# Head norms of the first block with tokens on partitions, half of one modulation sum on TensorE, the recurrent convolution accumulated in PSUM

## The chip, the cores and the metric

The kernel runs on one core of a Trainium2 chip. The metric is the device time of one execution in microseconds (us), taken as the median of several. TensorE is called PE in the profile, its weight load PEld, VectorE DVE, ScalarE ACT, GpSimd POOL and SyncE SP.

## The reference

Two transformer-like blocks run on 512 tokens of width 1024. The change lies wholly in the first part of the first block, ahead of its output projection:

```python
c_act = jax.nn.silu(c)
ada = c_act @ w_ada[l] + b_ada[l]
sh1, sc1, g1, sh2, sc2, g2 = jnp.split(ada, 6, axis=-1)
h = modulate(rmsnorm(x, norm1_g[l]), sh1, sc1)
z = h @ w_in[l]
gate_b, gate_c, xa, xr, gr = jnp.split(z, [CONV_W, 2 * CONV_W, 3 * CONV_W, 3 * CONV_W + LRU_W], axis=-1)
y_a = gate_b * causal_dwconv(gate_c * xa, conv_a_w[l])
xr = causal_dwconv(xr, conv_b_w[l]) + conv_b_b[l]
y_b = rg_lru(xr, w_r[l], b_r[l], w_i[l], b_i[l], lru_lambda[l]) * jax.nn.gelu(gr)
y = jnp.concatenate([head_rmsnorm(y_a, gn_a[l], N_CONV_HEADS),
                     head_rmsnorm(y_b, gn_b[l], N_LRU_HEADS)], axis=-1) @ w_out[l]
x = x + g1[:, None, :] * y
...
def head_rmsnorm(y, g, n_heads):
    yh = y.reshape(b, s, n_heads, w // n_heads).astype(jnp.float32)
    yh = yh * lax.rsqrt(jnp.mean(yh * yh, axis=-1, keepdims=True) + EPS)
    return yh.reshape(b, s, w).astype(y.dtype) * g
```

There are 16 heads of 64 channels, eight from each half. An expert layer with 16384 experts and a second block follow; nothing in them changes.

## The kernel before

**Layout and precision.** Activations lie with channels on the 128 partitions and the 512 tokens along the row. Width 1024 makes eight chunks of 128 channels, so a chunk of `y` holds two heads. Every large product is done in three passes: operand and weight are each split into a rounded upper part (`act_hi`, `w_hi`) and the rest (`act_lo`, `w_lo`).

**Units.** A unit is one block of 128 output channels: 24 matmuls of 512 columns (`linear`, L876; eight chunks by three passes). Its weights come by DMA into `raw`, ACT makes `w_hi` (`upper_part`, L1228, up to two units ahead), POOL makes `w_lo` (`lower`, L782). Units 0 to 19 are the projection `w_in`: 0 to 3 give `xr`, 4 to 7 `gr`, and 8 to 19 go round in threes (`z_of`, L643): `xa`, `gc` (gate_c), `gb` (gate_b). Units 20 to 27 are `w_out`.

**Order.** Each engine runs its own program strictly in the order written, and waits on semaphores. No scheduler reorders anything. PE, ACT and DVE each have a loop over the unit number u; numbers in tuples (`Y_SQUARE`, `Y_SUM`, `Y_SCALE`) say at which u a step of head chunk i is placed. These positions differ in time from engine to engine, since an engine can lag behind another by some units.

**Modulation sums.** The six vectors of `ada` are made in twelve halves. `weighted(h)` (L1623) on DVE sums eight products of a 128x512 piece of `w_ada` by a scalar into `acc`; `ada_half(h)` (L909) on PE turns `acc` into four columns with four matmuls against a column of ones. Halves 0 to 3 come before unit 0, half 4 after unit 3, half 5 after unit 5 (`ADA_AFTER`), 6 to 9 in the output projection. `ada_done` counts the finished halves.

**Recurrent half.** DVE convolves `xr` with four taps into `xc` (L1681, L1683), PE makes the two gates of chunk g after unit 5+g (L943, L944), ACT takes tanh, DVE does `recur_1(g)` (L1690, with one full reciprocal) at u=8 to 11, ACT takes four square roots, and DVE does `recur_2(g)` (L1704, with the scan, L1708) at u=13 to 16, which gives `y[4+g]`.

**Convolution half.** For each m, DVE multiplies `gc` by `xa` (L1727), convolves with three taps (L1731, L1733) and multiplies by `gb` (L1737), at u = 9, 12, 15, 18 and u = 10, 13, 16, 19.

**Head norm of chunk i** (order `Y_ORDER`): ACT squares `y` (L1242); PE multiplies the squares by the matrix `halves`, which sums each head over its 64 partitions and leaves the sum on every partition of the head, 128x512 (`squares`, L893, L902); ACT takes the root (L1248); DVE takes the reciprocal of all 128x512 elements (`invert`, L1589, L1594) and scales `y` (`scale_y`, L1711, L1718); ACT makes `act_hi` (`y_upper`, L1312, L1314) and DVE `act_lo` (L1755). On PE, the only step of this chain is the sum; what DVE does with it is awaited by PE only in that the next sum needs the root before (`rms_ready`) and in unit 20, chunk by chunk (`split=8`). After the eighth chunk DVE goes on to `weighted(6)`.

## Time and profile before

| | us |
|---|---|
| median of 3 runs | 2073.28 |
| the three runs | 2069.87, 2073.28, 2074.01 |
| the profiled execution | 2072.42 |
| its span, first to last instruction | 2070.7 |
| mean granted PE clock | 0.958 |
| PE busy / DVE busy | 1885.8 / 1673.6 |

The profiled execution took 0.86 us less than the median, and 1.7 us of it lie outside the span. All instants below are counted from the start of the span. The part that the change touches ends at about 217 us, a tenth of the span. The rest runs after it without a change: its first work needs what this part makes.

### The profile page before, as it was taken

What the parts mean: (1) busy time and instruction counts of PE and PEld (TensorE: products, weight loads), DVE (VectorE), ACT (ScalarE), POOL (GpSimd) and SP (SyncE); (2) the same over time, 40 slices, a digit from 0 to 9 for tenths busy, and PEclk for the clock granted to TensorE, in tenths of its full rate; (3) what the DMA queues carried; (4) which work ended last, traced back from release to release, by engine and by line L of the source; (5) the groups of instructions that cost most, each with busy time, mean ns of one, the idle gap of its engine ahead of it and who ended that gap; (6) DMA issues with size and microseconds to landing.
All of it is one profiled execution on the core that took longest, in us unless ns stands there. A gap on an engine that the chain in (4) does not pass through costs nothing. (4 is left out here: it accounts for less than half of the span.)

```text
span 2070.7 us, 27489 instructions
## 1 busy us (share of the span) xinstructions
PE 1885.8 (91%) x9551; PEld 1612.7 (78%) x9551; DVE 1673.6 (81%) x2614; ACT 712.8 (34%) x1101; POOL 1057.4 (51%) x654
## 2 busy tenths in 40 slices
PE   3997779999999999996699999999999888899996
PEld 2774558999998999996678787878787666788774
DVE  6889874999968888865789999999997977646646
ACT  2343134333334444432233333333334233233441
POOL 1332234555556556567777777777754622432102
PEclk7998789999999999998899999999999999999988
DMA  8241342555458889989999999999982221100011
GB/s 331 86 170 41 132 153 64 177 174 177 167 173 309 310 304 319 314 317 414 376 352 369 354 363 359 368 356 358 370 299 79 72 71 62 61 1 1 1 51 51
DMA packets 160807, 440.37 MB, mean 213 GB/s; under 512 B 13648, under 2 KB 63952, under 8 KB 157648
## 3 DMA queue, kind: packets, MB, share of 16 engines
q1 hardware_dynamic: 65296, 254.71, 34.6%
q0 software_dynamic: 36864, 134.23, 16.7%
q10 hardware_dynamic: 58560, 50.34, 7.4%
q8 instruction: 46, 0.75, 0.1%
q14 instruction: 41, 0.34, 0.0%
HBM read 386.80 MB, written 52.43 MB: 212 GB/s over the span
## 5 line engine op out<-in xcount | busy, mean ns | idle before, releaser
L786 POOL TENSOR_TENSOR w_lo<-raw,w_hi 128x1024 fp32r<-128x1024 f32 x300 | 724.8, 2416 | 835.7 <-ACT w_hi L1237 834.9
L1237 ACT ACTIVATE w_hi<-raw 128x1024 fp32r<-128x1024 f32 x332 | 351.7, 1059 | 973.6 <-PE PS L887 594.6
L887 PE MATMUL PS<-act_hi,w_hi 128*128 128x384 f32 (+1 forms) x1632 | 608.5, 373 | 72.5 <-POOL w_lo L786 38.9
L887 PE MATMUL PS<-act_hi,w_lo 128*128 128x384 f32 (+1 forms) x1632 | 592.0, 363 | 0.0
L887 PE MATMUL PS<-act_lo,w_hi 128*128 128x384 f32 (+1 forms) x1632 | 591.9, 363 | 0.0
L887 PEld LDWEIGHTS PS<-act_hi,w_hi 128*128 128x128 f32 x1632 | 315.5, 193 | 129.2 <-issue 38.5
L887 PEld LDWEIGHTS PS<-act_lo,w_hi 128*128 128x128 f32 x1632 | 314.7, 193 | 26.6
L887 PEld LDWEIGHTS PS<-act_hi,w_lo 128*128 128x128 f32 x1632 | 316.1, 194 | 24.5 <-issue 1.4
L1043 PE MATMUL PS<-w_hi,act_hi 128*128 128x512 f32 x768 | 302.6, 394 | 15.8 <-ACT arena L1353 6.7
L1043 PE MATMUL PS<-w_hi,act_lo 128*128 128x512 f32 x768 | 300.2, 391 | 0.0
L1043 PE MATMUL PS<-w_lo,act_hi 128*128 128x512 f32 x768 | 300.1, 391 | 0.0
L1925 DVE TENSOR_TENSOR act_lo<-arena,act_hi 128x384 fp32r<-128x384 f32 x128 | 236.9, 1851 | 32.7 <-ACT act_hi L1405 32.4
L1887 DVE CUSTOM_DVE_ANT_0 arena<-arena,PS 128x1024 f32<-128x1024 f32 x128 | 154.6, 1217 | 46.6 <-DMA arena<-in_expert_u_rows,arena 45.6
L1043 PEld LDWEIGHTS PS<-w_hi,act_hi 128*128 128x128 f32 x768 | 144.8, 189 | 56.2 <-issue 19.0
L1043 PEld LDWEIGHTS PS<-w_hi,act_lo 128*128 128x128 f32 x768 | 144.7, 188 | 30.7
L1043 PEld LDWEIGHTS PS<-w_lo,act_hi 128*128 128x128 f32 x768 | 145.0, 189 | 28.9
L1896 DVE SCALAR_TENSOR_TENSOR PS<-arena,PS 128x1024 f32<-128x1024 f32 x127 | 162.4, 1279 | 1.7
L832 POOL DMA_INDIRECT arena<-in_expert_v,arena x128 | 135.0, 1054 | 26.1 <-issue 20.7
L1877 DVE TENSOR_TENSOR arena<-PS,arena 128x1024 f32<-128x1024 f32 x96 | 117.2, 1221 | 35.6 <-PE PS L1006 29.9
L832 POOL DMA_INDIRECT arena<-in_expert_u_rows,arena x128 | 123.0, 961 | 29.9 <-issue 22.7
L1069 PEld LDWEIGHTS PS<-arena 128*128 128x128 f32 x752 | 89.1, 194 | 19.6 <-issue 10.1
L1069 PE MATMUL PS<-arena 128*128 128x128 f32 x752 | 94.9, 281 | 6.1 <-POOL arena L870 4.9
(309 smaller groups left out, 2074.4 us busy)
## 6 DMA issues: line engine op xcount, KB each, us to landing
raw<-in_expert_u SPq DMA_DIRECT2D x128, 512.0 KB
raw<-in_expert_v SPq DMA_DIRECT2D x128, 512.0 KB
raw<-in_w_in SPq DMA_DIRECT2D x52, 512.0 KB
arena<-in_w_ada SPq DMA_DIRECT2D x24, 1024.0 KB, 6.8
gel_d<-arena ACTq DMA_DIRECT2D x64, 384.0 KB
gates_d<-arena ACTq DMA_DIRECT2D x12, 2048.0 KB
arena<-gates_d SPq DMA_DIRECT2D x32, 768.0 KB
arena<-gel_d SPq DMA_DIRECT2D x32, 768.0 KB
```

The source lines that it names most:

```text
L786: pool.tensor_tensor(w_lo[:, k % SPLIT, :], raw[:, k % RAW, :], w_hi[:, k % SPLIT, :].bitcast(F32), ALU.subtract).then_inc(lo_split, 1)
L832: pool.indirect_dma_start(out=rows[buffer(s)], out_offset=None, in_=table, in_offset=bass.IndirectOffsetOnAxis(ap=row_i[:, s % SLOTS:s % S ...
L887: mm = pe.matmul(PS[:, bank, 0:n_tok], w[:, k % SPLIT, c * P:(c + 1) * P], x[:, c, 0:n_tok], start=(i == 0 and n == 0), stop=(i == KC - 1 ...
L1043: mm = pe.matmul(PS[:, 2 * q + half, :], coef(x, k)[:, q, :], w[:, k % SPLIT, own], start=(start and n == 0), stop=(stop and n == 2), skip ...
L1069: mm = pe.matmul(PS[:, b, h * P:(h + 1) * P], lhs(h), rhs(h), start=True, stop=True)
L1237: act.activation(w_hi[:, k % SPLIT, :], raw[:, k % RAW, :], ACT.Copy).then_inc(hi_split, 1)
L1877: chain.link(v.tensor_tensor(hot[:, n, :, :], numbers.unsqueeze(1).unsqueeze(1).to_broadcast([P, GROUP, 2, P]), routeT[:, 0:2, at].rearran ...
L1887: v.tensor_tensor_reduce(out=rows[buffer(s)], in0=rows[buffer(s)], in1=own_ps, scale=1.0, scalar=0.0, op0=ALU.mult, op1=ALU.add, accum_out ...
L1896: v.scalar_tensor_tensor(out=own_ps, in0=rows[buffer(s)], scalar=dots[:, k:k + 1], in1=own_ps, op0=ALU.mult, op1=ALU.add).then_inc(rows_us ...
L1925: v.tensor_tensor(coef(act_lo, b % 4), craw[:, b % 2, :].rearrange("p (q t) -> p q t", q=GT), coef(act_hi, b % 4).bitcast(F32), ALU.subtra ...
```

## The change

Four things change.

1. **Head norms.** PE now multiplies with the squares as the stationary operand and two columns of `halves` as the moving one: four matmuls of 2 columns for each chunk (`head_sum`), so the sums have tokens on the partitions and are 128x8. ACT's root and DVE's reciprocal become 128x8 (`head_root`, `head_invert`). Then ACT copies the 8 values out to 128x512 (`spread`), PE turns that back to channels on partitions with four matmuls of 128 columns against the identity (`head_spread`), and DVE scales `y` with that straight from PSUM. `head_spread(i)` stands in PE's program at `Y_INV[i]`, the u at which DVE had its reciprocal, and waits for ACT's `spread(i)`, which waits for DVE's `head_invert(i)`. DVE scales one step later.
2. **Half 2 of the modulation.** DVE sums four of its eight products; PE does the other four straight from the weights with 16 matmuls of one column, and DVE adds the two with one small instruction.
3. **Recurrent convolution.** The sum of the four taps lies in PSUM (banks 3, 4, 7, 7) until the last one writes `xc`.
4. **Order.** Convolutions 0 and 1 come ahead of `weighted(4)`, 2 and 3 ahead of `weighted(5)`. PE takes half 4 after unit 5 and half 5 after unit 7. The gates wait for two and four convolutions in place of one and two. The last lower parts of `y` are interleaved with the last scalings.

The core of the diff (semaphores, two small regions and SP's count of freed pieces are left out):

```diff
-        ADA_AFTER = {3: 4, 5: 5, U_OUT + 1: 6, U_OUT + 2: 7, U_OUT + 3: 8, U_OUT + 4: 9, U_Q + 2: 10, U_Q + 4: 11}
+        PE_SHARE = (2,)
+        ADA_AFTER = {5: 4, 7: 5, U_OUT + 1: 6, U_OUT + 2: 7, U_OUT + 3: 8, U_OUT + 4: 9, U_Q + 2: 10, U_Q + 4: 11}
...
-        Y_SCALE = (13, 16, 17, 18, 19, 20, 20, 20)
+        Y_INV = (13, 16, 17, 18, 19, 20, 20, 20)
...
+            def head_sum(i):
+
+                index, n = 1 + i, 8 + i
+                if index >= 2:
+                    pe.wait_ge(rms_ready, index - 1)
+                pe.wait_ge(sq_ready, n + 1)
+                pair = halves[:, :].rearrange("p (a b) -> p a b", a=2)[:, :, 0]
+                for q in range(TB):
+                    mm = pe.matmul(PS[:, 6 + index % 2, 2 * q:2 * q + 2], sq[:, n % 2, q * P:(q + 1) * P], pair,
+                                   start=True, stop=True)
+                mm.then_inc(sq_used, 1)
+                pe.wait_ge(sq_used, n + 1)
+                pe.nop().then_inc(sum_ready, 1)
+
+            def head_spread(i):
+
+                pe.wait_ge(spread_ready, i + 1)
+                if i >= 2:
+                    pe.wait_ge(y_scaled, i - 1)
+                for q in range(TB):
+                    mm = pe.matmul(PS[:, 3 + i % 2, q * P:(q + 1) * P], tmp[:, i % 2, q * P:(q + 1) * P], ident[:, :],
+                                   start=True, stop=True)
+                mm.then_inc(spread_ps, 1)
+
             def ada_half(h):
+                if h in PE_SHARE:
+                    pe.wait_ge(ada_in[(2 * h + 1) % 4], 16 * ((2 * h + 1) // 4 + 1))
+                    pe.wait_ge(c_ready, 1)
+                    for n in range(4):
+                        for c in range(4, KC):
+                            at = 512 * (c % 4) + n * P
+                            own = 40 + 4 * h + n
+                            mm = pe.matmul(PS[:, 5, own:own + 1], ada_w[:, (2 * h + 1) % 4, at:at + P], cs[:, c:c + 1],
+                                           start=(c == 4), stop=(c == KC - 1))
+                    mm.then_inc(ada_used_pe, 1)
...
@@ -932,7 +979,7 @@
...
-                    pe.wait_ge(xc_ready, g + 1)
+                    pe.wait_ge(xc_ready, (2, 4, 4, 4)[g])
...
                 for i in range(8):
                     if Y_SUM[i] == u:
-                        squares(8 + i, 1, 1 + i, halves)
-            for i in range(8):
-                if Y_SUM[i] == 20:
-                    squares(8 + i, 1, 1 + i, halves)
+                        head_sum(i)
+                    if Y_INV[i] == u:
+                        head_spread(i)
+            head_sum(6)
+            head_spread(5)
+            head_sum(7)
+            head_spread(6)
+            head_spread(7)
...
+            def head_root(i):
+                act.wait_ge(sum_ready, 2 + i)
+                if i >= 1:
+                    act.wait_ge(rinv_ready, i)
+                act.activation(hrms[:, i % 2, :], PS[:, 6 + (1 + i) % 2, 0:8], ACT.Sqrt, bias=eps,
+                               scale=1.0 / 64).then_inc(rms_ready, 1)
+
+            def spread(i):
+
+                act.wait_ge(rinv_ready, 2 + i)
+                if i >= 2:
+                    act.wait_ge(spread_ps, i - 1)
+                act.activation(tmp[:, i % 2, :].rearrange("p (a b) -> p a b", b=64),
+                               hinv[:, i % 2, :].unsqueeze(2).to_broadcast([P, 8, 64]), ACT.Copy).then_inc(spread_ready, 1)
...
                 for i in range(8):
                     if Y_SUM[i] == u:
-                        root(1 + i, 64)
+                        head_root(i)
+                    if Y_INV[i] == u:
+                        spread(i)
...
-            for i in range(5):
+            y_upper(0)
+            spread(5)
+            for i in range(1, 4):
                 y_upper(i)
-            root(7, 64)
-            y_upper(5)
-            root(8, 64)
-            y_upper(6)
-            y_upper(7)
+            head_root(6)
+            spread(6)
+            y_upper(4)
+            head_root(7)
+            spread(7)
+            for i in range(5, 8):
+                y_upper(i)
...
-                for c in range(KC):
+                for c in range(4 if h in PE_SHARE else KC):
...
             chain.link(v.tensor_tensor(ada[:, 0:16], PS[:, 5, 0:16], col("bada", 0, 16), ALU.add))
+            chain.link(v.tensor_tensor(ada[:, 8:12], PS[:, 5, 48:52], ada[:, 8:12], ALU.add))
             chain.link(v.scalar_tensor_tensor(out=gain1, in0=ada[:, 8:16], scalar=1.0, in1=col("n1", 0, 8),
                                               op0=ALU.add, op1=ALU.mult))
...
             for m in range(4):
-                if m < 2:
-                    weighted(4 + m)
                 dve.wait_ge(z_act, m + 1)
                 if m == 0:
                     dve.wait_ge(pool_made, 2)
                 w = [col("cbw", 4 * k + m) for k in range(4)]
-                chain.link(v.tensor_scalar(xc[:, m, :], xrp[:, m, 0:512], w[0], col("cbb", m), ALU.mult, ALU.add))
+                part = PS[:, (3, 4, 7, 7)[m], :]
+                if m == 3:
+                    dve.wait_ge(xc_ready, 3)
+                chain.link(v.tensor_scalar(part, xrp[:, m, 0:512], w[0], col("cbb", m), ALU.mult, ALU.add))
                 for k in range(1, 4):
-                    ins = v.scalar_tensor_tensor(out=xc[:, m, :], in0=xrp[:, m, k:k + 512], scalar=w[k],
-                                                 in1=xc[:, m, :], op0=ALU.mult, op1=ALU.add)
+                    ins = v.scalar_tensor_tensor(out=xc[:, m, :] if k == 3 else part, in0=xrp[:, m, k:k + 512], scalar=w[k],
+                                                 in1=part, op0=ALU.mult, op1=ALU.add)
                     if k < 3:
                         chain.link(ins)
                     else:
                         ins.then_inc(xc_ready, 1)
+                if m % 2:
+                    weighted(4 + m // 2)
...
+            def head_invert(i):
+
+                dve.wait_ge(rms_ready, 2 + i)
+                if i >= 2:
+                    dve.wait_ge(spread_ready, i - 1)
+                v.reciprocal(hinv[:, i % 2, :], hrms[:, i % 2, :]).then_inc(rinv_ready, 1)
+
             def scale_y(i):
 
                 c = Y_ORDER[i]
-                if i:
-                    invert(1 + i, i, y_scaled)
-                else:
-                    invert(1, 8)
-                v.scalar_tensor_tensor(out=y[:, c, :], in0=y[:, c, :], scalar=col("gn", c), in1=rinv, op0=ALU.mult,
-                                       op1=ALU.mult).then_inc(y_scaled, 1)
+                dve.wait_ge(spread_ps, i + 1)
+                v.scalar_tensor_tensor(out=y[:, c, :], in0=y[:, c, :], scalar=col("gn", c), in1=PS[:, 3 + i % 2, :],
+                                       op0=ALU.mult, op1=ALU.mult).then_inc(y_scaled, 1)
+
+            def lower_y(i):
+
+                dve.wait_ge(ahi_ready, 8 + i + 1)
+                v.tensor_tensor(act_lo[:, Y_ORDER[i], :], y[:, Y_ORDER[i], :], act_hi[:, Y_ORDER[i], :].bitcast(F32),
+                                ALU.subtract).then_inc(alo_ready, 1)
...
                 for i in range(8):
-                    if Y_SCALE[i] == u:
-                        scale_y(i)
+                    if Y_INV[i] == u:
+                        head_invert(i)
+                        if i:
+                            scale_y(i - 1)
...
-            for i in range(8):
-                if Y_SCALE[i] == 20:
-                    scale_y(i)
-
-                dve.wait_ge(ahi_ready, 8 + i + 1)
-                v.tensor_tensor(act_lo[:, Y_ORDER[i], :], y[:, Y_ORDER[i], :], act_hi[:, Y_ORDER[i], :].bitcast(F32),
-                                ALU.subtract).then_inc(alo_ready, 1)
+            head_invert(5)
+            scale_y(4)
+            for i in range(0, 3):
+                lower_y(i)
+            head_invert(6)
+            scale_y(5)
+            lower_y(3)
+            head_invert(7)
+            scale_y(6)
+            lower_y(4)
+            scale_y(7)
+            for i in range(5, 8):
+                lower_y(i)
```

On PE, from the head sum behind unit 12 to the one behind unit 15. L887 and L900 are the matmuls of a unit, of which only the first is shown, since it carries the unit's waits; `sq_ready` comes from ACT's square, `z_act` and `z_dve` free the unit's PSUM bank. Before:

```order
L902 MATMUL PS<-arena 128x512 [waits sq_ready,gates_th]
L887 MATMUL PS<-act_hi,w_hi 128x512 [waits sq_used,lo_split,z_dve]
...
L887 MATMUL PS<-act_hi,w_hi 128x512 [waits lo_split,z_act]
...
L887 MATMUL PS<-act_hi,w_hi 128x512 [waits lo_split,z_dve]
...
L902 MATMUL PS<-arena 128x512 [waits sq_ready,rms_ready]
L887 MATMUL PS<-act_hi,w_hi 128x512 [waits sq_used,lo_split,z_dve]
```

After (L930 is `head_sum`, L942 `head_spread`):

```order
L930 MATMUL PS<-arena 128x2 [waits sq_ready,gates_th]
L930 MATMUL PS<-arena 128x2 x3
L900 MATMUL PS<-act_hi,w_hi 128x512 [waits sq_used,lo_split,z_dve]
...
L942 MATMUL PS<-ident,arena 128x128 [waits spread_ready]
L942 MATMUL PS<-ident,arena 128x128 x3
L900 MATMUL PS<-act_hi,w_hi 128x512 [waits lo_split,z_act]
...
L900 MATMUL PS<-act_hi,w_hi 128x512 [waits lo_split,z_dve]
...
L930 MATMUL PS<-arena 128x2 [waits sq_ready,rms_ready]
L930 MATMUL PS<-arena 128x2 x3
L900 MATMUL PS<-act_hi,w_hi 128x512 [waits sq_used,lo_split,z_dve]
```

Behind unit 13 PE now has four matmuls that wait for `spread_ready`, and units 14 and 15 stand behind them.

On DVE, from the last product of `gb` 1 (L1737 before, L1823 after) to the next `gc`, where the first head norm is; L1707 to L1709 and L1783 to L1785 are `recur_2`. Before:

```order
L1737 TENSOR_TENSOR arena<-PS,arena 128x512 [waits unit_done,dve_chain]
L1707 TENSOR_TENSOR arena<-arena 128x512 [waits z_dve,root_ready]
L1708 SCALAR_TENSOR_TENSOR arena<-arena 128x512 [waits dve_chain]
L1709 TENSOR_TENSOR arena<-arena 128x512 [waits dve_chain]
L1594 RECIPROCAL arena<-arena 128x512 [waits tmp_ready,rms_ready]
L1718 SCALAR_TENSOR_TENSOR arena<-arena,cols 128x512 [waits rinv_ready]
L1707 TENSOR_TENSOR arena<-arena 128x512 [waits root_ready]
L1708 SCALAR_TENSOR_TENSOR arena<-arena 128x512 [waits dve_chain]
L1709 TENSOR_TENSOR arena<-arena 128x512 [waits dve_chain]
L1727 TENSOR_TENSOR arena<-PS,arena 128x512 [waits dve_chain,z_act,unit_done]
```

After:

```order
L1823 TENSOR_TENSOR arena<-PS,arena 128x512 [waits unit_done,dve_chain]
L1783 TENSOR_TENSOR arena<-arena 128x512 [waits z_dve,root_ready]
L1784 SCALAR_TENSOR_TENSOR arena<-arena 128x512 [waits dve_chain]
L1785 TENSOR_TENSOR arena<-arena 128x512 [waits dve_chain]
L1792 RECIPROCAL arena<-arena 128x8 [waits rms_ready]
L1783 TENSOR_TENSOR arena<-arena 128x512 [waits root_ready]
L1784 SCALAR_TENSOR_TENSOR arena<-arena 128x512 [waits dve_chain]
L1785 TENSOR_TENSOR arena<-arena 128x512 [waits dve_chain]
L1813 TENSOR_TENSOR arena<-PS,arena 128x512 [waits dve_chain,z_act,unit_done]
```

The large reciprocal and its scaling are gone from this place; a small reciprocal stands in it, still behind `recur_2(0)`, and the scaling of this chunk comes behind `recur_2(3)`.

## Rows read from the trace of the kernel before

**Rows 1.** stretches: us, PE, PEld, DVE, ACT, POOL busy (count), PE clock, DMA, GB/s

```profile
75.00:82.00 7.00, 6.02 (x23) 4.96 (x24) 6.50 (x7) 1.18 (x2) 2.38 (x1) 0.76 0.34 112
...
108.00:148.00 40.00, 39.70 (x169) 31.21 (x167) 35.56 (x29) 16.83 (x23) 14.07 (x7) 1.00 0.43 149
148.00:176.00 28.00, 25.37 (x103) 18.85 (x102) 26.86 (x22) 8.04 (x11) 12.21 (x5) 1.00 0.28 95
176.00:184.00 8.00, 4.19 (x9) 2.34 (x10) 7.79 (x6) 3.36 (x5) 2.36 (x1) 0.79 0.04 4
...
198.00:217.00 19.00, 9.19 (x22) 6.30 (x23) 16.81 (x14) 2.86 (x5) 0.00 (x0) 0.59 0.00 1
```

**Rows 2.** DVE, 119 to 217 us, by line: count | busy us, mean ns | idle

```profile
L1594 DVE RECIPROCAL arena<-arena 128x512 f32<-128x512 f32 x8 | 26.8, 3348 | 0.4 <-DVE arena L1737 0.2
```

**Rows 3.** DVE in order: start us, us, line, what, count [idle before <-releaser]

```profile
119.43 0.69 DVE L1727 TENSOR_TENSOR arena<-PS,arena 128x512 f32<-128x512 f32 x1 [2.81 <-PE PS L887]
...
146.26 3.53 DVE L1733 SCALAR_TENSOR_TENSOR arena<-arena,cols 128x512 f32<-128x512 f32 x2
...
154.50 3.35 DVE L1594 RECIPROCAL arena<-arena 128x512 f32<-128x512 f32 x1
...
215.98 0.69 DVE L1755 TENSOR_TENSOR act_lo<-arena,act_hi 128x512 fp32r<-128x512 f32 x1 [0.69 <-ACT act_hi L1314]
```

**Rows 4.** PE in order, same columns

```profile
75.98 1.05 PE L912 MATMUL PS<-ones,arena 128*128 128x1 f32 x8 [1.46 <-DVEq L1640]
...
142.18 0.39 PE L887 MATMUL PS<-act_lo,w_hi 128*128 128x512 f32 x1
...
147.62 0.39 PE L887 MATMUL PS<-act_lo,w_hi 128*128 128x512 f32 x1
...
179.51 1.75 PE L902 MATMUL PS<-arena 128*128 128x512 f32 x2 [3.85 <-ACT arena L1242]
```

**Rows 5.** DVE in the start

```profile
26.44 5.59 DVE L1635 SCALAR_TENSOR_TENSOR arena<-arena,small 128x512 f32<-128x512 f32 x7
32.27 3.35 DVE L1594 RECIPROCAL arena<-arena 128x512 f32<-128x512 f32 x1 [0.24 <-DVE arena L1635]
35.66 1.34 DVE L1633 TENSOR_SCALAR arena<-arena,small 128x512 f32<-128x512 f32 x1
```

**Rows 6.** POOL in order, the splits into w_lo

```profile
32.06 4.66 POOL L786 TENSOR_TENSOR w_lo<-raw,w_hi 128x1024 fp32r<-128x1024 f32 x2 [27.93 <-ACT w_hi L1237]
...
146.79 5.26 POOL L786 TENSOR_TENSOR w_lo<-raw,w_hi 128x1024 fp32r<-128x1024 f32 x2 [7.42 <-ACT w_hi L1237]
```

**Rows 7.** DVE, convolutions 0, 1 and 2, and a small reciprocal

```profile
58.29 0.18 DVE L1579 RECIPROCAL small<-small 128x4 f32<-128x4 f32 x1
...
76.09 2.34 DVE L1681 TENSOR_SCALAR arena<-arena,cols 128x512 f32<-128x512 f32 x1 [0.32 <-DVE arena L1635]
...
89.66 4.33 DVE L1683 SCALAR_TENSOR_TENSOR arena<-arena,cols 128x512 f32<-128x512 f32 x3
...
94.48 2.33 DVE L1683 SCALAR_TENSOR_TENSOR arena<-arena,cols 128x512 f32<-128x512 f32 x3
```

**Rows 8.** DVE, expert stage, 1060 to 1500 us, by line: operations with PSUM and without

```profile
L1925 DVE TENSOR_TENSOR act_lo<-arena,act_hi 128x384 fp32r<-128x384 f32 x106 | 197.7, 1865 | 23.1 <-ACT act_hi L1405 22.9
L1896 DVE SCALAR_TENSOR_TENSOR PS<-arena,PS 128x1024 f32<-128x1024 f32 x114 | 145.8, 1279 | 1.6
...
L1900 DVE TENSOR_SCALAR PS<-arena 128x1024 f32<-128x1024 f32 x1 | 1.3, 1289 | 0.1
```

**Rows 9.** PE, second block: 16 passes of 128 columns, at either clock

```profile
1766.43 1.95 PE L1069 MATMUL PS<-arena 128*128 128x128 f32 x16
...
1808.33 3.50 PE L1069 MATMUL PS<-arena 128*128 128x128 f32 x16 [4.87 <-POOL arena L870]
```

**Rows 10.** ACT, 0 to 230 us, by line

```profile
L1237 ACT ACTIVATE w_hi<-raw 128x1024 fp32r<-128x1024 f32 x24 | 25.4, 1057 | 77.0 <-PE PS L887 72.8 <-DMA raw<-in_w_in 4.3
...
L1242 ACT ACTIVATE arena<-arena 128x512 f32<-128x512 f32 x8 | 5.0, 625 | 3.1 <-DVEq L1739 3.1
```

More of the change, by code:

```diff
@@ L291, in build @@
         rinv = region("rinv", 27672, 1, 512)[:, 0, :]
+        hrms = region("hrms", 30040, 2, 8)
+        hinv = region("hinv", 30056, 2, 8)
         lru_q = region("lru_q", 28184, 1, 512)[:, 0, :]
@@ L401, in build @@
         ada_used = sem("ada_used")
+        ada_used_pe = sem("ada_used_pe")
         ada_acc = sem("ada_acc")
@@ L436, in build @@
         y_scaled = sem("y_scaled")
+        spread_ready = sem("spread_ready")
+        spread_ps = sem("spread_ps")
         x_ready = sem("x_ready")
@@ L628, in lowered, with piece_used @@
             return lo_split, u + 1 - N_KEYS // 4
+        def piece_used(i):
+            if i % 2 and i // 2 in PE_SHARE:
+                return ada_used_pe, PE_SHARE.index(i // 2) + 1
+            return ada_used, sum(1 for n in range(i + 1) if not (n % 2 and n // 2 in PE_SHARE))
         def coef(x, k):
@@ L660, in ada_half @@
                     if i >= 4:
-                        sp_.wait_ge(ada_used, i - 3)
+                        sp_.wait_ge(*piece_used(i - 4))
                     sp_.dma_start(ada_w[:, i % 4, :], A["w_ada"][h][:, 2048 * (i % 2):2048 * (i % 2) + 2048]
```

## The prediction

> **What bounds the kernel now.** The stage table [rows 1] comes first. From 108 to 176 us PE and DVE both look full: PE is busy 39.70 of 40 us and DVE 35.56, then 25.37 and 26.86 of 28. Behind 176 us PE has holes and DVE none: 4.19 us of PE against 7.79 of DVE in 8 us, and from 198 to 217 us 9.19 against 16.81, with PE's granted clock down to 0.59. So DVE sets the end of this part. The list of DVE's groups says with what: eight reciprocals of 128x512 at 3348 ns, 26.8 us in all [rows 2]. DVE in order of time gives the instants: it last waits for PE at 119.43 us, comes to the first head reciprocal at 154.50 and ends its last lower part at 215.98 + 0.69 = 216.67 us [rows 3]. That end is my yardstick. Four sums `weighted(6)` to `weighted(9)` follow on DVE at once and pace the output projection, so a shift of this instant passes to the end of the program; nothing behind it is changed.
>
> PE in order of time gives the other half. A unit takes 147.62 - 142.18 = 5.44 us, and unit 13 ends at 142.4 us [rows 4]. DVE comes to the head reciprocal that belongs to unit 13's place only at 154.50 [rows 3]. **PE runs 12 us ahead of DVE there.** Today this lead costs nothing: PE goes on with units 14 and 15, and DVE finds them done.
>
> **The start (half 2).** DVE drops four of eight products; seven take 5.59 us [rows 5], so 4 x 0.80 = 3.2 us. But POOL makes its first two splits at 32.06 us, 4.66 us for both [rows 6], and before they ran beside the reciprocal at 32.27 us, which they don't slow; only the next instruction lost time, 1.34 us against about 0.5 [rows 5]. Moved 3.2 us forward, `weighted(3)` starts under these splits. One split costs a product with two SBUF operands about 2 us: three convolution steps took 4.33 us with a split beside them and 2.33 without [rows 7]. Two splits cost about 4 us in place of 0.85, which eats the 3.2. The added small instruction costs 0.2. PE's 16 products are 32 passes, at 1.05 / 8 us each [rows 4] 4.2 us, twice that at half clock, and PE has from 27 to 43 us for them. I take 0 for the start, with -3.2 (no collision) and +0.4 as its ends.
>
> The Trainium skill (SBUF — State Buffer, SBUF: two separate sides) says that GpSimd and a VectorE operation with two SBUF inputs, or in a two-port mode, lock each other out for the whole instruction. By that rule the start gains 0, without it 3.2 us; the convolution rows just named agree with the rule.
>
> **Convolutions in PSUM and the new order.** A step with one operand in PSUM isn't held up by POOL: 114 of 1024 columns average 1279 ns in a stage where the product without PSUM takes 1865 ns for 384 columns [rows 8]. Half of 1279 is 0.64 us, near the 0.78 of an undisturbed step now [rows 7]. The first step rises from about 0.55 to 1289 / 2 = 0.64 us [rows 8], and two stalls of 2 us on DVE go [rows 7]. None of it is on the path by itself, because DVE waits for PE behind the convolutions.
>
> The Trainium skill (VectorE: DVE Perf Modes, Why PSUM operands drop a tier) speaks against the first step: a PSUM operand excludes the mode with two reads. By the page it doubles from about 0.5 us; by the rows it costs 0.1 us more, 0.4 us for four.
>
> What counts is the order. PE waits 1.46 us for half 4 behind unit 3 [rows 4], and its clock then falls: 0.76 over the next 7 us [rows 1] is 1.7 us lost. With the half behind unit 5 DVE has it ready (about 82 us, PE asks at 85.5), and the gates find their convolutions (DVE at 73.5 and 88, PE at 86 and 93.5). **Gain 3.2 us**: unit 9 ends at 116.2 us in place of 119.4, unit 13 at 139.2. Ends: 1.5 to 3.5.
>
> **The head norms.** DVE loses 8 x (3.35 - 0.2) = 25.2 us; 0.2 is a small reciprocal [rows 7]. Prices of the new chain, all hot: small reciprocal 0.25 with its wait, ACT's copy 0.63 [rows 10], 0.7 with its wait; `head_spread` is 8 passes of 128 columns, 16 took 1.95 us [rows 9], so 1.1 with its wait; `head_sum` is 8 passes of 2 columns, like the 1.05 of [rows 4], with its own wait 1.3 (today also about 1.3); ACT's small root 0.3.
>
> `head_spread(0)` stands behind unit 13 on PE and waits for DVE's `head_invert(0)`, still behind `recur_2(0)`. Queued behind it are units 14 and 15, which DVE needs for `gc` 2. ACT waits too, in `spread`, with its split for unit 16 behind. In turn:
>
> 1. DVE starts `gc` 0 at 116.2. Up to the reciprocal it needed 154.50 - 119.43 = 35.1 us [rows 3], with two POOL splits in it [rows 6]; one of them now can't come, since ACT is stuck: 33. `head_invert(0)` at 149.3, `head_spread(0)` at 150.2. **PE idle 11 us** (9 to 13).
> 2. Spread 1.1, units 14 and 15 10.9: 162.2. DVE did `recur_2(1)` in 2.6 us and idled 10.
> 3. `gc` 2: 2.8 and 2.0 for a split (two steps took 3.53 beside one, 1.5 without [rows 3, 6]): 167.0. `recur_2(2)` 169.6. PE: sum 1.3, unit 16: 169.0. `gb` 2 and `recur_2(3)` with a partial stall 5.1: 174.7. Invert and copy: 175.7. PE idle 6.7.
> 4. Spread, sum, unit 17: 1.1 + 1.3 + 5.5: 183.6. ACT first splits weights (1.06 [rows 10]) and copies `xa`, then spreads: 185.8. PE idle 2.2.
> 5. Spread, sum, unit 18: 193.7. DVE idled about 14 us. `gc` 3 with a split 4.8, invert and copy 0.9: 199.4. PE idle 5.7.
> 6. Spread, sum, unit 19: 207.3; `gb` 3 and invert: 208.4.
> 7. Tail: three rounds of invert, copy, spread, sum, root, 3.65 each, and 3.3 for the last scaling and lower parts: **222.7 us**.
>
> Against 216.67 this is +6.0 us with PE always at full clock. DVE gave up 25.2 us of work and got more than 34 us of waiting.
>
> **The clock.** 3.85 us of idleness ahead of 179.51 [rows 4] went with a clock of 0.79 over 8 us [rows 1]: 1.7 us lost, as above. Four stalls: 4 x 1.7 = 6.8. In the tail two PE steps a round take 3.50 / 1.95 of their time at the lower of the two levels (1.2 of 2.4 GHz) [rows 9], about 0.8 more each, six steps: 4.7; I take half, 2.3. **Sum: +6.0 + 6.8 + 2.3 = +15 us** on the profiled 2072.4, so 2087.5; the median lay 0.9 above the profiled execution, and the cold share of the second and third stall may overlap, so I say 2087 for the median.
>
> **Rivals.** *The reciprocals' time comes through* (faster). If DVE reached `head_invert(0)` before 139.2 us, PE would never wait. PE's own floor is 139.2 + 6 x 5.5 + 8 x (1.3 + 1.1) = 191.4 us, 196 with the last lower parts: -21 us, 2052. For it: 26.8 us of reciprocals are truly on DVE's path [rows 2]. Against it: DVE would have to be 10 us earlier at `recur_2(0)`, and nothing ahead of that place gets shorter but the 3.2 us that PE gains as well. 5%. Part of it (short stalls, -4 to -15 us) 4%.
>
> *The waits replace the gain, nothing more* (no change). With sum and spread at half their prices (0.5 each less, eight times each, some 6 of them on the path: -6), a start that gains its 3.2 and a PE that keeps its clock, the sum is between -3 and +3: 2070 to 2077. 11%.
>
> *Coupled more tightly* (slower still). Every spread and sum at half clock (+0.8 each on about 12) and a POOL split in each `recur_2`: +22 to +28, 2095 to 2101. 13%.
>
> My forecast (+4 to +22, 2077 to 2095) has 67%. The change not doing what it says isn't a case: each of the moved instructions stands in the new order.
>
> **Numbers.** About 0.2% (4 us) is what a measurement of this kernel can tell from no change. Faster 0.09; within 0.2% 0.11; slower 0.80. The range leaves out the faster case and the far end of the tight one: 2074 to 2097.
>
> **What would show it.** In the profile after: PE idle ahead of `head_spread` 0, 1 and 3, released by ACT's copy, 11, 7 and 6 us; DVE idle ahead of `gc` 2, `gc` 3 and `gb` 3 that wasn't there; small reciprocals of 0.2 us; unit 9 about 3 us earlier than now; `weighted(2)` half as long and `weighted(3)` slowed by POOL; PE's clock under 0.85 in the slices from 150 to 215 us; last lower part at about 231 us. It is wrong if `head_spread(0)` finds its data, if DVE is busy between 150 and 195 us, or if unit 13 ends later than `recur_2(0)`.

## The result and the profile after

| | before | after |
|---|---|---|
| median, us | 2072.47 (4 runs, 2069.87 to 2074.01) | 2093.6 (4 runs, 2092.01 to 2096.89) |
| profiled execution, us; its span | 2072.42; 2070.7 | 2096.89; 2095.2 |
| ratio | | 1.0105, 95% interval 1.0088 to 1.0123 |
| last lower part of the head norms ends (DVE) | 216.67 | 234.85 + 1.89 = 236.74 (DVE's next instruction, at 236.65, overlaps it a little) |

The change makes the kernel 21 us slower. The profiled execution is the slowest of the four; of the 24.5 us between it and the one of before, 20.1 stand at the yardstick instant of the prediction (the end of DVE's last lower part). The unchanged part behind that instant took 1854.0 us before and 1858.5 after, and between 1851.0 and 1856.9 in the profiled executions below; so a median can lie some us off what its yardstick says. The stage table of the kernel after, columns as in [rows 1]:

```profile
75.00:82.00 7.00, 7.00 (x32) 5.80 (x31) 6.71 (x6) 3.08 (x4) 3.40 (x2) 1.00 0.34 111
108.00:148.00 40.00, 30.61 (x135) 24.40 (x133) 32.84 (x30) 15.90 (x22) 14.40 (x6) 0.94 0.37 126
148.00:176.00 28.00, 19.94 (x88) 16.56 (x88) 15.87 (x16) 5.49 (x8) 7.15 (x3) 0.87 0.17 47
176.00:192.00 16.00, 12.10 (x40) 9.97 (x40) 2.39 (x6) 3.18 (x6) 0.64 (x1) 0.64 0.08 31
192.00:208.00 16.00, 9.48 (x41) 7.72 (x42) 5.60 (x6) 2.76 (x5) 4.05 (x2) 0.79 0.19 60
208.00:222.00 14.00, 11.84 (x51) 10.06 (x50) 1.58 (x4) 2.47 (x4) 1.93 (x1) 0.74 0.02 7
222.00:237.00 15.00, 13.34 (x58) 12.60 (x58) 8.63 (x16) 7.88 (x16) 0.42 (x1) 0.55 0.01 1
```

Where [rows 1] had a full DVE, DVE now works 15.87 of 28 us, then 2.39 of 16, 5.60 of 16 and 1.58 of 14. PE isn't full either, and its granted clock lies between 0.55 and 0.87. Neither engine bounds this stretch; they wait for each other in turn. In the first row, which had 0.76 before, the granted clock is 1.00: PE's wait for half 4 behind unit 3 is gone. PE's side, its five waits ahead of the spreading passes (in brackets the idle time ahead of a row, and who ended it):

```profile
150.51 2.08 PE L942 MATMUL PS<-ident,arena 128*128 128x128 f32 x8 [11.60 <-ACT arena L1314]
...
177.71 2.08 PE L942 MATMUL PS<-ident,arena 128*128 128x128 f32 x8 [6.95 <-ACT arena L1314]
...
192.34 1.16 PE L942 MATMUL PS<-ident,arena 128*128 128x128 f32 x8 [2.23 <-ACT arena L1314]
...
207.67 2.07 PE L942 MATMUL PS<-ident,arena 128*128 128x128 f32 x8 [5.88 <-ACT arena L1314]
...
220.68 1.16 PE L942 MATMUL PS<-ident,arena 128*128 128x128 f32 x8 [1.86 <-ACT arena L1314]
```

DVE's side, in order of time: the product sums at the start, a convolution in PSUM, `gc` 0 (it answers to 119.43 in [rows 3]), the first head inverse, `gc` 2, `gc` 3, `gb` 3, the last three lower parts:

```profile
34.65 7.54 DVE L1707 SCALAR_TENSOR_TENSOR arena<-arena,small 128x512 f32<-128x512 f32 x7
...
84.17 0.81 DVE L1755 TENSOR_SCALAR PS<-arena,cols 128x512 f32<-128x512 f32 x1 [0.25 <-DVE arena L1707]
85.02 1.55 DVE L1757 SCALAR_TENSOR_TENSOR PS<-arena,cols,PS 128x512 f32<-128x512 f32 x2
...
115.82 0.69 DVE L1813 TENSOR_TENSOR arena<-PS,arena 128x512 f32<-128x512 f32 x1 [5.92 <-PE PS L900]
...
149.61 0.19 DVE L1792 RECIPROCAL arena<-arena 128x8 f32<-128x8 f32 x1
...
163.99 0.69 DVE L1813 TENSOR_TENSOR arena<-PS,arena 128x512 f32<-128x512 f32 x1 [11.64 <-PE PS L900]
...
201.83 0.69 DVE L1813 TENSOR_TENSOR arena<-PS,arena 128x512 f32<-128x512 f32 x1 [19.30 <-PE PS L900]
...
218.86 0.69 DVE L1823 TENSOR_TENSOR arena<-PS,arena 128x512 f32<-128x512 f32 x1 [11.29 <-PE PS L900]
...
234.85 1.89 DVE L1804 TENSOR_TENSOR act_lo<-arena,act_hi 128x512 fp32r<-128x512 f32 x3
```

DVE is 3.6 us early at `gc` 0, comes to the first inverse without a wait, and then idles 11.64, 19.30 and 11.29 us for units that are queued behind PE's waits.

### The profile page after: what moved, and what is told of

It reads as the page before. It is cut to its first block, busy times and chain, and to the rows that moved or that the text cites. A ratio compares the mean times of both kernels' runs of the same rounds, so it can differ in the third digit from the quotient of the medians.

```text
span 2095.2 us, 27792 instructions
## 1 busy us (share of the span) xinstructions
PE 1905.5 (91%) x9695; PEld 1641.3 (78%) x9695; DVE 1643.9 (78%) x2611; ACT 714.2 (34%) x1109; POOL 1054.5 (50%) x654
## 4 chain that ended last, share of the span: by engine, by line
PE 70%; DVE 14%; POOL 5%; issue 5%; DMA 4%; ACT 2%; ACTq 0%; SPq 0%; DVEq 0%; PEldq 0%; POOLq 0%
PE PS L900 35%; PE PS L1094 18%; PE PS L1120 4%; PE PS L1057 4%; POOL w_lo L799 3%; DVE arena L1707 2%; POOL arena L845 2%; DVE arena L2122 2%; DMA gates_d<-arena 1%; DVE arena L1666 1%; PE PS L1266 1%; PE PS L1248 1%; DVE PS L1990 1%; DMA raw<-in_expert_u 1%; PE PS L915 1%
## 5 line engine op out<-in xcount | busy, mean ns | idle before, releaser
L900 PE MATMUL PS<-act_hi,w_hi 128*128 128x384 f32 (+1 forms) x1632 | 608.3, 373 | 59.2 <-POOL w_lo L799 37.0
L900 PE MATMUL PS<-act_hi,w_lo 128*128 128x384 f32 (+1 forms) x1632 | 593.1, 363 | 0.0
L900 PE MATMUL PS<-act_lo,w_hi 128*128 128x384 f32 (+1 forms) x1632 | 591.6, 363 | 0.0
L900 PEld LDWEIGHTS PS<-act_hi,w_hi 128*128 128x128 f32 x1632 | 316.2, 194 | 107.5 <-POOL w_lo L799 33.2
L900 PEld LDWEIGHTS PS<-act_lo,w_hi 128*128 128x128 f32 x1632 | 315.6, 193 | 26.6
L900 PEld LDWEIGHTS PS<-act_hi,w_lo 128*128 128x128 f32 x1632 | 316.1, 194 | 24.5 <-issue 1.4
L1094 PEld LDWEIGHTS PS<-w_lo,act_hi 128*128 128x128 f32 x768 | 144.7, 188 | 28.9
```

Of the source, the lines that this page charges most:

```text
L900: mm = pe.matmul(PS[:, bank, 0:n_tok], w[:, k % SPLIT, c * P:(c + 1) * P], x[:, c, 0:n_tok], start=(i == 0 and n == 0), stop=(i == KC - 1 ...
L1094: mm = pe.matmul(PS[:, 2 * q + half, :], coef(x, k)[:, q, :], w[:, k % SPLIT, own], start=(start and n == 0), stop=(stop and n == 2), skip ...
```

## The experiments

Theory: the loss is made by the place at which PE waits (its lead over DVE is given up), and is paid a second time in PE's clock. Rivals: the new small work itself is dear; the other three parts cost something; the units are late for another reason. In the table "last lower" is the end of DVE's last lower part in the profiled execution (before 216.67); ratios are to the kernel before on the same chip, with 95% intervals. The experiments ran on three chips, on which the kernel before took 2072.27, 2073.46 and 2072.30 us, so differences of about 1 us between medians of two chips mean nothing.

| kernel | median, us | ratio | last lower |
|---|---|---|---|
| changed kernel again | 2093.24 | 1.0104 (1.0087 to 1.0121) | 237.85 |
| old head norms, the other three parts | 2068.65 | 0.9985 (0.9975 to 0.9995) | 210.90 |
| new head norms alone | 2096.95 | 1.0124 (1.0107 to 1.0141) | 242.04 |
| late spreading | 2055.84 | 0.9925 (0.9903 to 0.9946) | 197.95 |
| copies of constants | 2071.12 | 0.9994 (0.9979 to 1.0009) | 218.78 |
| copies of constants, first in ACT's queue | 2054.19 | 0.9908 (0.9892 to 0.9925) | 198.72 |
| useless passes, short | 2091.94 | 1.0090 (1.0074 to 1.0105) | 233.50 |
| useless passes, full | 2081.24 | 1.0046 (1.0032 to 1.0060) | 225.23 |
| first weight split held | 2092.68 | 1.0101 (1.0086 to 1.0117) | 237.14 |
| new order alone | 2070.17 | 0.9985 (0.9976 to 0.9994) | 213.37 |
| late spreading, `weighted(6)` moved | 2056.00 | 0.9919 (0.9904 to 0.9934) | 200.47 |

**Which part costs.** The changed kernel with its norms undone, and the reverse. Of the first, the scalings on DVE (PE's and ACT's steps are put back as well):

```diff
-                    if Y_INV[i] == u:
-                        head_invert(i)
-                        if i:
-                            scale_y(i - 1)
+                    if Y_SCALE[i] == u:
+                        scale_y(i)
```

> The kernel before with half 2 shared, the convolutions in PSUM and the new order, but with the old head norms (full reciprocals, sums on all 128 partitions). My theory, that the loss is all in the head norms: gc 0 starts on DVE at about 116 us, as in the changed kernel, DVE is busy from there as before, and its last lower part ends about 3.5 us earlier than 216.67, so about 2069 us. Rival, that the lead of PE hides the earlier start or that the PSUM operands cost what they save: 2072 to 2074. Rival, that these three parts themselves carry part of the loss: above 2076.

Measured 2068.65, 3.6 us under the 2072.27 of before; `gc` 0 starts at 115.64. The three other parts gain, and gain what was forecast. The reverse, from the changed kernel:

```diff
-        PE_SHARE = (2,)
-        ADA_AFTER = {5: 4, 7: 5, ...
+        PE_SHARE = ()
+        ADA_AFTER = {3: 4, 5: 5, ...
...
-                part = PS[:, (3, 4, 7, 7)[m], :]
```

> The changed kernel with half 2, the convolutions and their order as they were before; only the head norms are new. My theory: the first stall of PE, ahead of the first spreading passes, is again 11 us, only about 3.5 us later in time, the following stalls are the same, and the whole is about 3.5 us slower than the changed kernel: 2096 to 2098 us. Rival, that the stalls come from units that arrive earlier than DVE can use them: the first stall is then about 8 us and the time stays at 2092 to 2094.

Measured 2096.95, 3.7 above the changed kernel, with PE's first wait 12.0 us and its five waits 28.9 us in all (28.5 in the changed kernel). The parts add up. The norms alone cost 24.6 us (2093.24 - 2068.65), or 24.7 against the kernel before on one chip (2096.95 - 2072.27).

**Is it the place of the wait?** Same work, spreading passes later in PE's order, copies and scalings with them, the tail interleaved to fit:

```diff
+        Y_SPREAD = (16, 17, 18, 19, 20, 20, 20, 20)
+        Y_SCALE = (17, 18, 19, 20, 20, 20, 20, 20)
...
 PE
-                    if Y_INV[i] == u:
+                    if Y_SPREAD[i] == u:
                         head_spread(i)
...
 ACT, ahead of its wait for the unit
+                for i in range(8):
+                    if Y_SPREAD[i] == u:
+                        spread(i)
```

> The changed kernel with the same work, but the spreading passes of head norm 0 stand behind unit 16 on PE in place of unit 13, those of 1 to 3 behind units 17 to 19, the others in the tail; ACT's copies and DVE's scalings move with them. My theory, that what costs is the place at which PE waits in its order and not the new work: PE has no wait above 3 us ahead of the spreading passes, its clock stays near full, unit 19 ends at about 184 us and the last lower part at 197 to 200, so 2053 to 2058 us, faster than both kernels. Rival, that the small passes and copies themselves are dear (sums and spreads at twice their price): PE is busy all through and the last lower part ends at about 215, 2070 us. Rival, that DVE again sets the end (scalings and lower parts in the tail): the last lower part at 205 to 210, 2062 to 2067.

Measured 2055.84, **16 us faster than before and 37 faster than the changed kernel**. PE in order of time in this kernel (L944 is `head_spread`):

```profile
158.21 1.06 PE L944 MATMUL PS<-ident,arena 128*128 128x128 f32 x8
...
167.45 1.16 PE L944 MATMUL PS<-ident,arena 128*128 128x128 f32 x8 [1.38 <-ACT arena L1317]
...
175.24 1.06 PE L944 MATMUL PS<-ident,arena 128*128 128x128 f32 x8
...
182.95 1.06 PE L944 MATMUL PS<-ident,arena 128*128 128x128 f32 x8
```

Of the 28.5 us of waits ahead of spreading passes 0 to 4, one of 1.38 us and a gap of 0.30 are left. The rival of dear small work falls: all of it is still there. But this kernel changes two things: PE's wait comes later, and ACT's copies stand ahead of the next weight split. Spreading passes moved on PE alone were not tried.

**Whose wait is it?** The order of the changed kernel, but ACT copies constants in place of the inverses, so the head norms are missing from the values:

```diff
-                act.wait_ge(rinv_ready, 2 + i)
...
-                               hinv[:, i % 2, :].unsqueeze(2)...
+                               col("gn", 0, 8).unsqueeze(2)...
```

> The changed kernel in its own order, but ACT's copy spreads eight columns of constants in place of the inverses that DVE makes, so it waits for nobody on DVE; the head norms are left out of the values in this way, and all instructions stay. My theory: with this one dependence gone PE's stalls ahead of the spreading passes vanish, the last lower part ends at about 198 us and the whole takes 2053 to 2060 us. Rival, that the new work itself costs the time: 2085 to 2093. Rival, that PE then stalls at the next dependence on DVE (the square of the next head tile) as long as before: 2080 or more.

Measured 2071.12, outside every expectation. PE still waits 12.2 us for the copies, though these need nothing of DVE. ACT in order of time shows why for the first of them:

```profile
134.65 1.66 ACT L1378 ACTIVATE arena<-arena 128x512 f32<-128x512 f32 x3
141.41 0.63 ACT L1378 ACTIVATE arena<-arena 128x512 f32<-128x512 f32 x1 [5.09 <-DVE arena L1776]
141.94 1.04 ACT L1288 ACTIVATE w_hi<-raw 128x1024 fp32r<-128x1024 f32 x1
142.89 0.61 ACT L1313 ACTIVATE arena<-cols 128x512 f32<-128x512 f32 x1
```

The copy (L1313) is queued behind a square root that waits for DVE's `recur_1(3)` and behind a weight split. The four later waits, 1.75 us and once 2.23, have a weight split of 1.06 us ahead of the copy, the one of 2.23 also ACT's copy of `xa`; the changed kernel has that 2.23 too, so it was none of DVE's there. So a second coupling lay under the first. Moved ahead of both (the old place is deleted):

```diff
 ACT, ahead of its wait for unit u
+                for i in range(8):
+                    if min(Y_INV[i], 20) == u + (1 if i == 0 else 0) and u < 20:
+                        spread(i)
```

> The kernel whose ACT copies spread constants (the head norms left out of the values), and in it these copies 0 to 4 moved on ACT ahead of the next weight split, copy 0 ahead of the four square roots too; PE's order is the one of the changed kernel. My theory, that what was left of PE's waits there, 12.2 us, stood behind ACT's own queue (a square root that waits for DVE, a weight split of 1.06 us): no wait above 1 us ahead of spreading passes 0 to 4, the last lower part ends at 198 to 203 in place of 218.78, 2054 to 2059 us. Rival, that PE then waits as long for another step of DVE (a bank that the product of three units earlier must free): last lower part at 212 or later, 2065 or more.

Measured 2054.19; one wait of 2.0 us is left on PE ahead of passes 0 to 4, for a bank that a scaling must free. Of the 39 us between this kernel and the changed one, the medians give 22 to the data from DVE (2093.24 - 2071.12) and 17 to ACT's queue (2071.12 - 2054.19), the last lower parts 19 and 20 (237.85, 218.78, 198.72). The kernel in the middle spreads from 2066 to 2078 us, so no finer split than about half and half is shown, and only in this order of undoing: with the real inverses in place, an earlier place in ACT's queue alone was not tried.

**What does the clock cost?** Useless passes on PE ahead of its waits:

```diff
             def head_spread(i):
+                for n in range((30, 16, 4, 14, 0, 0, 0, 0)[i]):
+                    pe.matmul(PS[:, 5, 128:256], ones[:, :], ident[:, :], start=True, stop=True)
                 pe.wait_ge(spread_ready, i + 1)
```

> The changed kernel, with 30, 16, 4 and 14 useless passes of 128 columns on PE (0.29 us each at the high clock, into a corner of bank 5 that nobody reads) ahead of its waits for the spreading passes 0 to 3. They take 8.7, 4.6, 1.2 and 4.1 us, less than the waits of 11.60, 6.95, 2.23 and 5.88 us, so they delay nothing. My theory, that the stalls cost a second time because PE's clock falls behind them: the clock stays at full from 150 to 208 us, unit 17 takes 5.5 us in place of 8.5, the last lower part ends 9 to 12 us earlier than 236.65, and the whole takes 2081 to 2085 us. Rival, that the units are long behind the stalls for another reason (weights or splits that arrive late): 2091 to 2095. Rival, that the passes come in the way of the spreading passes: above 2096.

Measured 2091.94, which looks like the first rival, but the experiment wasn't what I meant: a useless pass (one matmul of 128 columns, two passes in the profile's count) took 6.86 / 30 = 0.229 us, not 0.29, so PE stood idle behind them for 4.94 us, and the first spreading passes ran at the lower level all the same (2.08 us):

```profile
138.62 6.86 PE L939 MATMUL PS<-ident,ones 128*128 128x128 f32 x60
150.42 2.08 PE L944 MATMUL PS<-ident,arena 128*128 128x128 f32 x8 [4.94 <-ACT arena L1316]
```

Its last lower part, 233.50, is 3.2 and 4.4 us earlier than in the two profiled executions of the changed kernel, but the median gains only 1.3. With every wait only part filled, it decides nothing about the clock. Again with 49, 29, 9 and 24 passes:

> The changed kernel with 49, 29, 9 and 24 useless passes of 128 columns on PE ahead of its waits for the spreading passes 0 to 3. In the run with 30, 16, 4 and 14 of them one took 0.229 us and not 0.29, and PE still stood idle for 4.94, 3.39, 1.34 and 2.76 us; now they take 11.2, 6.6, 2.1 and 5.5 us and fill the waits of the changed kernel nearly whole. My theory, that an idle PE costs a second time through its clock: no idle time above 0.6 us ahead of these spreading passes, the granted clock at 0.95 or more from 150 to 208 us, unit 17 takes 5.5 us, the last lower part ends at 225 to 229 in place of 236.65, the whole takes 2082 to 2087 us. Rival, that the clock is not what makes the units long: last lower part at 233 or later, 2090 to 2095. Rival, that useless passes of this kind don't hold the clock: granted clock below 0.85 in those stretches, 2090 to 2095.

Measured 2081.24, **12.0 us less than the changed kernel**, with the same useful work; that is a little below the range of the theory, and its other signs came (last lower part 225.23, clock 1.00). PE by order of time, then the stage table, in this kernel:

```profile
138.80 11.10 PE L939 MATMUL PS<-ident,ones 128*128 128x128 f32 x98
150.57 1.16 PE L944 MATMUL PS<-ident,arena 128*128 128x128 f32 x8 [0.67 <-ACT arena L1316]
...
176.42 1.16 PE L944 MATMUL PS<-ident,arena 128*128 128x128 f32 x8 [0.49 <-ACT arena L1316]
...
186.59 1.16 PE L944 MATMUL PS<-ident,arena 128*128 128x128 f32 x8 [0.22 <-ACT arena L1316]
...
200.45 1.16 PE L944 MATMUL PS<-ident,arena 128*128 128x128 f32 x8 [0.53 <-ACT arena L1316]
```

```profile
148.00:176.00 28.00, 26.96 (x163) 23.64 (x162) 17.18 (x19) 5.75 (x9) 7.16 (x3) 1.00 0.19 63
176.00:192.00 16.00, 14.75 (x88) 12.95 (x89) 1.14 (x3) 4.00 (x8) 2.35 (x1) 1.00 0.11 36
192.00:208.00 16.00, 15.17 (x100) 13.59 (x98) 5.61 (x6) 2.48 (x4) 2.35 (x1) 1.00 0.10 34
208.00:222.00 14.00, 10.48 (x56) 9.93 (x55) 7.08 (x15) 8.56 (x17) 2.35 (x1) 0.70 0.00 0
```

These passes bring PE its data no earlier. But the granted clock is 1.00 where it was 0.87, 0.64 and 0.79, and the units behind the waits are shorter. That a low clock made the units long is shown by this. From 208 us, where nothing was filled, it falls as before. The yardstick on the same chip:

> The changed kernel again, unchanged, as the yardstick on the same chip for the two others: 2091 to 2097 us, the waits ahead of the spreading passes 11.6, 7.0, 2.2 and 5.9 us, the last lower part at 236 to 238. If it stands below 2090, the small differences of the kernels with useless passes and with the late split must be read anew.

Measured 2093.24, with the same five waits, 28.5 us.

**The start.** POOL's first split held until `weighted(3)` is made:

```diff
+            pool.wait_ge(ada_acc, 4)
             for u in range(U_Q):
                 lower(u, u)
```

> The changed kernel with POOL's first weight split held until DVE has made weighted(3). My theory of the start, that the two first splits slow weighted(3) by about 2 us each and so eat what half 2 saves: the seven products behind the reciprocal take 5.6 us in place of 7.54, normed starts 2 to 3 us earlier than 44.91, and the whole is 2 to 3 us faster, 2090 to 2092. Rival, that the splits only move and slow normed as much: unit 0 ends where it did, 2093 to 2095. Rival, that unit 0 then waits for its weights: slower, 2096 or more.

Measured 2092.68, not to be told from 2093.24. DVE in order of time in this kernel, the sum and the first two steps of the norm behind it, then PE in order of time, its first pass of unit 0:

```profile
33.99 5.59 DVE L1708 SCALAR_TENSOR_TENSOR arena<-arena,small 128x512 f32<-128x512 f32 x7
...
42.30 3.38 DVE L1672 SCALAR_TENSOR_TENSOR arena<-xres,small,arena 128x512 f32<-128x512 f32 x2
```

```profile
46.78 0.76 PE L901 MATMUL PS<-act_hi,w_hi 128*128 128x512 f32 x1 [5.13 <-DVE act_lo L1680]
```

The sum falls from 7.54 to 5.59 us and the norm starts 2.6 us earlier (42.30, was 44.91), but now its first two steps stand beside the splits: 3.38 us in place of 1.42. So 2.0 of the 2.6 us are lost again, and unit 0 starts 0.65 us earlier (was 47.43). The splits for the most part only move, as the first rival said.

**Order or PSUM?** The kernel before with the new order alone (`ADA_AFTER` and the places of `weighted(4)` and `weighted(5)`; the convolutions stay in SBUF):

```diff
-                if m < 2:
-                    weighted(4 + m)
...
+                if m % 2:
+                    weighted(4 + m // 2)
```

> The kernel before with the new order alone: convolutions 0 and 1 ahead of weighted(4), 2 and 3 ahead of weighted(5), the halves on PE behind units 5 and 7; convolutions accumulate in SBUF as before. My theory, that the order brings nearly all of the 3.6 us and PSUM little: no wait behind unit 3 on PE, gc 0 starts on DVE at 116 to 117 us, 2068.5 to 2070. Rival, that without PSUM the splits of POOL hold the convolutions and the gates wait for them: gc 0 at 118 to 120, 2071 to 2073.

Measured 2070.17 with `gc` 0 at 118.13: the instant is the rival's, the time stands at the edge of the theory's. The two rows of `gc` 0, of this kernel and of the one with all three parts:

```profile
118.13 0.69 DVE L1727 TENSOR_TENSOR arena<-PS,arena 128x512 f32<-128x512 f32 x1 [6.66 <-PE PS L887]
```

```profile
115.64 0.69 DVE L1750 TENSOR_TENSOR arena<-PS,arena 128x512 f32<-128x512 f32 x1 [5.92 <-PE PS L896]
```

In these executions the order brings 1.3 of 3.8 us, PSUM and half 2 the other 2.5. Of these, 0.96 stand at the start of unit 0 already (48.21 against 47.25), and that is in part chance: with the old start, unit 0 began at 47.67 in the kernel before and at 47.64 in the one with the new norms alone. Another 1.0 are waits that the order left on PE, 0.54 and 0.47 us ahead of halves 4 and 5; the kernel with all three parts has neither. DVE, then PE, with the new order alone, a first step of a convolution in SBUF beside a split of POOL, and half 4:

```profile
70.97 2.63 DVE L1679 TENSOR_SCALAR arena<-arena,cols 128x512 f32<-128x512 f32 x1
```

```profile
86.49 1.05 PE L912 MATMUL PS<-ones,arena 128*128 128x1 f32 x8 [0.54 <-DVEq L1640]
```

In the changed kernel a step in PSUM beside such a split took 0.81 us. The ratios, 0.9985 for both kernels, don't tell them apart, so the part of PSUM in the time is not shown.

**Further?** In the kernel with late spreading, DVE's idle time is used for `weighted(6)`:

```diff
+                if u == 17:
+                    chain.wait()
+                    weighted(6)
```

> The kernel with the late spreading passes, and in it weighted(6) taken out of the head of the output projection and put into the 8 us for which DVE waited ahead of gc 3. My theory, that DVE has become idle there and paces the output projection behind: DVE's first sum of the output projection comes 5 us earlier (about 201 in place of 206.23), PE's units then limit, and the whole is 2 to 5 us faster than with late spreads alone, 2051 to 2054. Rival, that the moved sum delays gc 3 and with it unit 19 and the last head norm: 2055 to 2059.

Measured 2056.00, no gain that can be told (the four runs without the move lie between 2051.55 and 2059.26). DVE in this kernel, its first sum of the output projection, then `weighted(7)` and the second sum:

```profile
203.52 0.75 DVE L1883 SCALAR_TENSOR_TENSOR xres<-PS,ada,xres 128x512 f32<-128x512 f32 x1 [3.05 <-PE PS L902]
...
204.70 10.00 DVE L1712 SCALAR_TENSOR_TENSOR arena<-arena,small 128x512 f32<-128x512 f32 x7
214.94 0.75 DVE L1883 SCALAR_TENSOR_TENSOR xres<-PS,ada,xres 128x512 f32<-128x512 f32 x1 [0.24 <-DVE arena L1712]
```

The first sum comes 2.7 us earlier (was 206.23), but `weighted(7)` now takes 10.00 us (was 7.61), and the second sum stands at 214.94, where it was 215.27. The time is the rival's, its reason only in part: `gc` 3 starts as before (175.56, was 175.44), but `gb` 3 is 1.2 us late (184.38, was 183.15) and the last lower part 2.5. What the first sum gained all the same went in the next one. There two of POOL's splits (at 204.74 and 210.18) now fall into the 10.00 us, where one (at 208.67) fell into the 7.61. This fits the price of about 2 us for each; no kernel tests it.

## Why the prediction was right, point by point

Forecast 2087 (2074 to 2097, slower at 80%), measured 2093.6: the sign and the range hold, and the point is 6.6 us low. At the yardstick 231.8 was forecast (216.67 + 15.1) and 236.74 measured; of these 4.9 us, 3.7 are the clock behind the stalls, 1.1 the sum at full clock, 0.2 the tail. The rest of the 6.6, 1.7, is no more than the part behind the yardstick varies from one execution to the next.

- **The mechanism** stood as said: waits on PE of 11.60, 6.95, 2.23 and 5.88 us where 11, 6.7, 2.2 and 5.7 were forecast; `head_invert(0)` at 149.61 (149.3), `head_spread(0)` at 150.51 (150.2). DVE's waits came at the three places named. The late and the uncoupled kernels show that PE's waits are the cause.
- **The sum with a hot PE** (at full clock throughout) was right too, and the filled kernel is its test: spreading passes 1, 2 and 3 at 176.42, 186.59 and 200.45 us, forecast 175.7, 185.8 and 199.4. Its last lower part, 225.23, is 2.5 later than 222.7, of which 1.1 stood already ahead of the tail (`gb` 3 at 208.42 against 207.3).
- **The clock term was mis-sized**: 6.8 + 2.3 = 9.1 us for stalls and tail. Measured, 236.74 - 222.7 = 14.0 is left for it and for the 1.1 just named, and the filled kernel shows 11.5 of that as clock by experiment (12.6 against the second profile of the changed kernel). The tail's 2.3 was right: from `gb` 3 to the last lower part 17.9 us (218.86 to 236.74), forecast 15.4 hot (207.3 to 222.7). The step that failed was "four stalls at 1.7 each", taken from one stall of 3.85 us in [rows 4]: 6.8 us forecast, 10.5 and 11.8 measured. From the instants above, first and second execution of the changed kernel against the filled one: from `head_spread(0)` to `gc` 2 1.4 and 2.1 us lost, from spreading 1 to spreading 2 4.5 and 3.2, from 2 to 3 1.5 and 3.0, from 3 to `gb` 3 3.2 and 3.5. The mean is 2.8, not 1.7. The instants of the second execution:

```profile
150.69 2.08 PE L942 MATMUL PS<-ident,arena 128*128 128x128 f32 x8 [11.60 <-ACT arena L1314]
...
178.61 2.08 PE L942 MATMUL PS<-ident,arena 128*128 128x128 f32 x8 [6.95 <-ACT arena L1314]
...
191.99 1.44 PE L942 MATMUL PS<-ident,arena 128*128 128x128 f32 x8 [2.23 <-ACT arena L1314]
...
208.83 2.08 PE L942 MATMUL PS<-ident,arena 128*128 128x128 f32 x8 [5.88 <-ACT arena L1314]
```

- **The start** was taken at 0 and is -0.25 us (unit 0 at 47.43, before 47.67), which is within what executions of one start differ by. The collision with POOL was as forecast (7.54 us for seven products beside two splits, 5.59 without). The Trainium skill (SBUF — State Buffer, SBUF: two separate sides) has GpSimd and a VectorE operation with two SBUF inputs lock each other out; the held split agrees: the 2 us went wherever the splits went (7.54 to 5.59, 1.42 to 3.38).
- **Convolutions and order**: 3.2 us forecast, 3.6 measured at `gc` 0, confirmed by the kernel with the old norms. The split of it is open: I gave PSUM nothing, and at `gc` 0 the new order alone brought 1.3, but by the ratios it brought all. Halving the times of 1024 columns was a wrong reading: the first step in PSUM takes 0.81 us where 0.64 was forecast and 0.55 stood before, and the later ones 0.78 (1.55 / 2), not 0.64. The Trainium skill (VectorE: DVE Perf Modes, Why PSUM operands drop a tier) has it lose the doubled rate; the direction agrees, and the whole instruction takes 1.5 times as long here, not twice.
- **The rivals.** "The reciprocals' time comes through", 2052, got 5% for this order and didn't come; with the wait placed later (2055.84), or with no data to wait for and the copy first (2054.19), the time comes to within 4 us of it. "Coupled more tightly" from 2095 on has its profile in part: most spreads and sums of the tail ran at half clock (0.55 from 222 to 237 us), though without a POOL split in each `recur_2`. Step 4 of the sum had ACT's split ahead of one copy (2.2 us). I missed that ACT's queue was a coupling at every wait: in the kernel without data from DVE 12.2 us of waits stayed.

## What to carry to other kernels

An engine that runs ahead of another owns a lead that costs nothing; before an instruction on it is made to wait for the slower one, compare the instants at which each comes there, and put the step behind as many units as the lead has (here the lead of 12 us is a little over two units; the step stood three units later, with ACT's copies ahead of its splits, and the kernel went from 21 us slower to 16 faster with the same work; other distances were not tried). Then look at the queue of the engine that carries the data between them, since it can hold the step as long as the data do. Price a stall on PE at its length and at what the units behind it lose in clock, and take that from more than one stall.

## What the runs showed of the hardware

- PE's idle time cost 12 us beyond its own length, and useless matmuls of 128 columns (0.229 us each) in its place held the granted clock at 1.00 and gave the 12 us back (2093.24 to 2081.24).
- What a stall costs in clock doesn't follow its length: the longest, 11.60 us, cost least (1.4 and 2.1 us), the one of 6.95 us 4.5 and 3.2, the one of 2.23 us 1.5 and 3.0. Why is open.
- 4.94 us of idleness behind 6.86 us of useless passes left the next passes at the lower level of the two (2.08 us against 1.16), as the whole wait of 11.60 us did.
- A VectorE instruction that reads SBUF alone and writes PSUM ran beside a GpSimd split without loss (0.81 us, as away from one); the same step from SBUF to SBUF took 2.63 us there in place of 0.54.
